# A third projection unit with its own buffers, and a hybrid attention/RWKV-7 kernel as one stretch instead of three

## The chip, the core and the metric

The kernel runs on one core of a Trainium2 chip. A core has TensorE (PE, matrix products into the PSUM banks), VectorE (DVE), ScalarE (ACT), GpSimd (POOL) and SyncE (SP, which here issues almost all DMA). Each runs its own instruction stream in order; they meet through semaphores. The metric is the device time of one execution in microseconds (us), lower is better. The median of three executions is given, and one further execution was profiled.

## The reference

`T` is 528 (16 meta tokens ahead of 512), `D` is 1024, 16 heads of 64, `D_FF` is 2816, all in fp32. Layer 0 mixes by stick-breaking attention, layer 1 by RWKV-7; each is followed by a SwiGLU.

```python
def swiglu(h, w_in, w_out):
    gate, up = jnp.split(jnp.einsum('btd,df->btf', h, w_in), 2, axis=-1)
    return jnp.einsum('btf,fd->btd', jax.nn.silu(gate) * up, w_out)

# attention, for each block of 128 queries
z = jnp.einsum('bhtd,bhsd->bhts', qb, kb).astype(jnp.float32) * scale
log_rest = jnp.where(mask, jax.nn.log_sigmoid(-z), 0.0)
later = lax.cumsum(log_rest, axis=3, reverse=True) - log_rest
att = jnp.where(mask, jnp.exp(jax.nn.log_sigmoid(z) + later), 0.0)
outs.append(jnp.einsum('bhts,bhsd->bhtd', att.astype(vb.dtype), vb))
...                                     # o: the outs put together
return jnp.einsum('btd,de->bte', o, w_o), v

# RWKV-7, after projections and small low-rank products
def step(S, inp):
    r_t, w_t, k_t, v_t, a_t, b_t = inp
    sa = jnp.einsum('bhij,bhj->bhi', S, a_t)
    S = (S * w_t[:, :, None, :] + sa[..., None] * b_t[:, :, None, :]
         + v_t[..., None] * k_t[:, :, None, :])
    return S, jnp.einsum('bhij,bhj->bhi', S, r_t)
...
y = ((y - mean) * lax.rsqrt(var + GN_EPS) * ln_x_w + ln_x_b)      # per head
bonus = jnp.sum(r_h * k_h * r_k, axis=-1, keepdims=True) * v_h
return jnp.einsum('btd,de->bte', (y + bonus) * g, w_o)

# the whole
for i in range(DEPTH):                  # DEPTH is 2; mix: attention, then RWKV-7
    h = h + mix
    h = h + swiglu(rms_norm(h, ffn_norm[i]), w_ffn_in[i], w_ffn_out[i])
return rms_norm(h[:, N_META:], final_norm)
```

## The kernel before

All activations are held with features on the partitions: 8 rows ("m" or "t", 0 to 7) of 128 features by the tokens. Every large product is made of *units*: a unit is 128 output features of one weight, so 1024 x 128 weights for the projections. fp32 accuracy comes from splitting each factor in a high and a low part and summing three products, hi x hi, lo x hi and hi x lo. A unit passes through five hands:

- SP loads it (`unit_load`, L770 ff) into `w_raw`, one of two buffers, unit u into buffer u % 2.
- ACT rounds it to `w_hi` (`split_hi`, L131), DVE subtracts for `w_lo` (`split_lo`, L135), again two buffers each.
- PE multiplies, for each row t, three matmuls for each stretch of columns (two stretches of 264 in layer 0, one of 512 in layer 1).
- DVE evicts the result from its PSUM bank; for a projection this is the residual addition (L1378), which frees the bank.

A buffer may be loaded again when both splits are made, and split again when PE is through with the unit that had it (`unit_done`).

The program is three `nc.Block`s. Each block has five functions, one for each engine, and at its end all engines meet before one of them enters the next:

1. Attention, first MLP half (`Mlp`, n = 0) and the front of the RWKV layer (`Front`: its projections and the tables of the recurrence).
2. The chunk stage (`chunk_stage`): the recurrence in chunks of 64 tokens.
3. `Output` (norm of each head, bonus, gate) and the second MLP half with the final norm (`Mlp`, n = 1).

Both MLP halves begin with the 8 units of the output projection `w_o`. The products of units 0 and 1 are woven into the stage ahead: as soon as a row of the attention output `o_hi`/`o_lo` (in layer 1 `x_hi`/`x_lo`) exists, PE multiplies it with both units. Unit 2 is split after unit 0 is done, since it has the same `w_hi`, `w_lo` buffers, and so on, in turn:

```python
        for m in range(KT):
            if m < 2:
                self.first.finish_out(pe, self, m)
                continue
            u = begin(m)
            products(m, range(KT), b.o_hi, b.o_lo, KT).then_inc(k.unit_done[u % 2].h, 1)
```

At the end of attention the last row exists only after the last pair of heads, so PE waits for `o_lo`, issues that row for units 0 and 1 (12 matmuls) and then unit 2. In `Output.tensor` a round m is: variance product of m, the head sums of m + 1, and the products of row m - 2 with units 0 and 1; rows 6 and 7 stand behind the loop.

The front needs constants: a mask over heads, two selection matrices `pick` and `put`, the chunk stage's masks. POOL makes them at the start of `Front.gpsimd` (L2572 ff), while PE is in the first units of the front. There ACT and DVE split v, the first projection's weights and the sums of the mixed inputs (L2033 and L2039).

In the chunk stage's block SP loads the two first units of `w_o`, then, when the gate is done, the residual `res` that the front had moved to DRAM, and waits for it ahead of the block's end:

```python
                sp.dma_start(k.res[:], k.res_kept).then_inc(res_in.h, 16)
                sp.wait_ge(res_in.h, 16)
```

Unit 2 and 3 of `w_o` are loaded behind that meeting, the units from 4 on when the buffers come free. The last front instruction on DVE is the product `bk` (L2570); the chunk stage's DVE stream begins with clearing `state` (L3044) and the product `neighbours` (L3056), on which PE's first chunk product (L3225) waits.

## Time and profile before

| | |
|---|---|
| median of 3 executions | 1543.97 us (1540.83 to 1547.42) |
| profiled execution, its own time | 1547.64 us |
| its span in the profile | 1545.7 us |
| TensorE busy | 1484.7 us, 96% of the span, 15443 matmuls |
| VectorE busy | 1024.0 us, 66% |
| ScalarE busy | 746.5 us, 48% |
| GpSimd busy | 104.9 us, 7% |
| DMA | 127.71 MB, mean 83 GB/s |
| mean granted TensorE clock | 0.992 of full |

The span runs from the first to the last instruction in the profile, and is 1.94 us shorter than the execution's own time. Busy times hold neither branches and semaphore instructions nor the issuing of DMAs. Matmuls are pipelined, so two neighbouring ones overlap in the profile, and the distance of their starts is what each costs. A timeline row has the start in us, the duration, engine, line, operation and tiles, and in brackets the idle time of that engine just ahead of it with what ended it; PEq is PE's sequencer. The granted clock is 1.00 at 2.4 GHz and 0.50 at 1.2 GHz.

### The profile page before, as it was taken

To read this page: it belongs to the slowest core of one execution; us is meant where nothing else is said; L and a number is where in the kernel's file an instruction comes from. 1 tells how busy PE (TensorE), PEld (TensorE's weight loads), DVE (VectorE), ACT (ScalarE), POOL (GpSimd) and SP (SyncE) were. 2 spreads that over 40 slices of the span, in tenths; PEclk is the share of its full clock that TensorE was granted. 3 is DMA by queue.
4 is the path that set the end of the run, shared out by engine and by line. 5 is a ranking of instruction groups with operands and counts; after the bars stand their busy time and mean duration, and the time that the engine had idled before them with its cause. 6 is when DMAs were issued, how large, how long until landed. Compare 5 with 4: busy or idle time off the path is not lost. (4 is left out here: it accounts for less than half of the span.)

```text
span 1545.7 us, 35328 instructions
## 1 busy us (share of the span) xinstructions
PE 1484.7 (96%) x15443; PEld 1364.5 (88%) x15443; DVE 1024.0 (66%) x1435; ACT 746.5 (48%) x1090; POOL 104.9 (7%) x145
## 2 busy tenths in 40 slices
PE   6999999999999999998999999999889999999997
PEld 6988898899999999998998788888558899899986
DVE  5675675687734886587788755545678885478732
ACT  4655555444522555467588433333344553245522
POOL 3110010000000001500000410101000000000010
PEclk9999999999999999998999999999999999999999
DMA  4212212324432333563222200000322434334331
GB/s 127 69 49 76 63 56 63 110 82 110 121 89 79 110 100 95 155 198 108 83 66 84 67 3 4 5 4 4 113 68 82 122 90 116 100 93 110 84 94 55
DMA packets 226840, 127.71 MB, mean 83 GB/s; under 512 B 8536, under 2 KB 221680, under 8 KB 226432
## 3 DMA queue, kind: packets, MB, share of 16 engines
q1 hardware_dynamic: 226384, 125.39, 28.3%
q8 instruction: 122, 2.00, 0.5%
q14 instruction: 30, 0.25, 0.1%
q10 hardware_dynamic: 304, 0.08, 0.0%
HBM read 119.03 MB, written 6.42 MB: 81 GB/s over the span
## 5 line engine op out<-in xcount | busy, mean ns | idle before, releaser
L131 ACT ACTIVATE w_hi<-w_raw 128x1024 fp32r<-128x1024 f32 (+1 forms) x124 | 143.8, 1160 | 221.1 <-PE psg L1844 115.4
L135 DVE TENSOR_TENSOR w_lo<-w_raw,w_hi 128x1024 fp32r<-128x1024 f32 (+1 forms) x123 | 167.9, 1366 | 69.8 <-ACT w_hi L131 69.7
L1844 PE MATMUL psg<-mid_hi_l,w_hi 128*128 128x264 f32 (+1 forms) x552 | 179.7, 325 | 3.1 <-DVE w_lo L135 2.2
L1844 PE MATMUL psg<-mid_lo_l,w_hi 128*128 128x264 f32 (+1 forms) x552 | 178.3, 323 | 0.0
L1844 PE MATMUL psg<-mid_hi_l,w_lo 128*128 128x264 f32 (+1 forms) x552 | 177.8, 322 | 0.0
L1844 PEld LDWEIGHTS psg<-mid_hi_l,w_hi 128*128 128x128 f32 x552 | 104.4, 189 | 12.2 <-DVE w_lo L135 2.8
L1844 PEld LDWEIGHTS psg<-mid_lo_l,w_hi 128*128 128x128 f32 x552 | 104.5, 189 | 8.0 <-issue 0.2
L1844 PEld LDWEIGHTS psg<-mid_hi_l,w_lo 128*128 128x128 f32 x552 | 104.5, 189 | 7.9
L2640 PE MATMUL psg<-x_hi,w_hi 128*128 128x264 f32 (+1 forms) x320 | 100.7, 315 | 7.1 <-DVE w_lo L135 7.1
L1378 DVE TENSOR_TENSOR res<-res,psg 128x512 f32<-128x512 f32 (+1 forms) x38 | 26.3, 692 | 119.2 <-PE psg L1844 103.5
L2640 PE MATMUL psg<-x_lo,w_hi 128*128 128x264 f32 (+1 forms) x320 | 99.7, 311 | 0.0
L2640 PE MATMUL psg<-x_hi,w_lo 128*128 128x264 f32 (+1 forms) x320 | 99.5, 311 | 0.0
L2640 PEld LDWEIGHTS psg<-x_hi,w_hi 128*128 128x128 f32 x320 | 61.8, 193 | 11.3 <-DVE w_lo L135 8.1
L1687 PE MATMUL psx<-t_hi_l,x_sums_hi_l 128*128 128x264 f32 (+1 forms) x240 | 67.7, 282 | 0.0
L1687 PE MATMUL psx<-t_lo_l,x_sums_hi_l 128*128 128x264 f32 (+1 forms) x240 | 67.7, 282 | 0.0
L1687 PE MATMUL psx<-t_hi_l,x_sums_lo_l 128*128 128x264 f32 (+1 forms) x240 | 67.5, 281 | 0.0
L2640 PEld LDWEIGHTS psg<-x_hi,w_lo 128*128 128x128 f32 x320 | 61.9, 193 | 2.7
L2640 PEld LDWEIGHTS psg<-x_lo,w_hi 128*128 128x128 f32 x320 | 61.8, 193 | 2.5
L582 PE MATMUL psg<-x_hi,w_hi 128*128 128x264 f32 x200 | 60.6, 303 | 2.6 <-DVE w_lo L135 2.2
L1090 ACT ACTIVATE x_sums_hi_l<-x_sums_l 128x1024 fp32r<-128x1024 f32 x40 | 41.9, 1057 | 33.9 <-DVE x_sums_l L1267 33.9
L582 PE MATMUL psg<-x_hi,w_lo 128*128 128x264 f32 x200 | 57.6, 288 | 0.0
L582 PE MATMUL psg<-x_lo,w_hi 128*128 128x264 f32 x200 | 57.3, 286 | 0.0
(517 smaller groups left out, 4767.6 us busy)
## 6 DMA issues: line engine op xcount, KB each, us to landing
w_raw<-in_w_ffn_out_dram SPq DMA_DIRECT2D x40, 704.0 KB, 4.6
w_raw<-in_w_qkv_dram SPq DMA_DIRECT2D x24, 512.0 KB, 3.8
w_raw<-in_w_rkv_dram SPq DMA_DIRECT2D x24, 512.0 KB, 4.1
x_raw_l<-in_w_ffn_in_dram SPq DMA_DIRECT2D x18, 512.0 KB, 4.2
x_raw_l<-in_w_ffn_in_dram SPq DMA_DIRECT2D x36, 256.0 KB, 4.8
w_raw<-in_w_ffn_in_dram SPq DMA_DIRECT2D x16, 512.0 KB, 3.8
y_raw_l<-in_w_ffn_in_dram SPq DMA_DIRECT2D x16, 512.0 KB, 4.1
y_raw_l<-in_w_ffn_in_dram SPq DMA_DIRECT2D x32, 256.0 KB, 4.7
```

Source lines behind the costliest of these rows:

```text
L131: k.nc.scalar.activation(k.w_hi[j][:, 0:kt, :], k.raw[j][:, 0:kt, :], ACT.Copy).then_inc(k.hi_ready[j].h, 1)
L135: k.nc.vector.tensor_tensor(k.w_lo[j][:, 0:kt, :], k.raw[j][:, 0:kt, :], k.w_hi[j][:, 0:kt, :].bitcast(F32), ALU.subtract).then_inc(k.lo_r ...
L582: done = mm(out, w[:, t, :], x, start=t == 0 and n == 0, stop=t == KT - 1 and n == 2)
L1090: self.k.nc.scalar.activation(p.s_hi[:, part], p.s[:, part], ACT.Copy).then_inc(self.s.high_s.h, 1)
L1378: nc.vector.tensor_tensor(row, row, self.psum(i % 2), ALU.add).then_inc(self.freed(i), 1)
L1687: done = self.k.nc.tensor.matmul(out, w[:, t, :], x_part[:, t, :], start=start and t == 0 and n == 0, stop=t == KQ - 1 and n == 2, skip_gr ...
L1844: done = k.nc.tensor.matmul(self.bank(i, c), w[:, t, :], x, start=t == 0 and n == 0, stop=t == count - 1 and n == 2)
L2640: done = nc.tensor.matmul(k.psg[:, 2 * j + c, 0:size], w[:, t, :], x[:, at:at + size], start=t == 0 and a == 0, stop=t == KT - 1 and a == 2)
```

## The change

**A third unit.** Unit 2 of `w_o` gets buffers of its own (`third_hi`, `third_lo`) and a PSUM bank of its own in both MLP halves, so neither waits for units 0 and 1. ACT splits it in the last pair of heads ahead of its eviction of `o_hi`, and in `Output` in round 0 between the square and the logarithm; DVE splits it ahead of `o_lo`, and in `Output` behind `product(2)`. At the end of attention PE multiplies rows 0 and 1 of unit 2 (12 matmuls), then the last row of units 0 and 1, then rows 2 to 7. At the end of `Output` rows 5 to 7 of units 0 and 1 stand behind the loop; ahead of them PE multiplies rows 0 to 4 of unit 2 (15), behind them rows 5 to 7 (9). The buffers of the units that follow are assigned as before, the PSUM banks of some are exchanged (`slot`).

**Constants.** `Front.constants` stands in POOL's stream of the first MLP half now, behind the release of the last of that half's paired units; only the cast of `put` stays at the start of the front. Four tiles (`put_raw`, `raw_first`, one hi and one lo tile of the paired weights) have other addresses.

**One block.** One `nc.Block` holds all stages. `chunk_stage` returns its five functions instead of running them. In place of the meetings stand semaphores: `c_first_v` and `c_first_p` (DVE's and POOL's last front products), `psum_free` of the front's last unit ahead of the first chunk products, and the chunk stage's own `y_r` and `bk_r` ahead of `Output`. SP still waits for `res` before it goes on to the units 2 and 3 of `w_o`.

```diff
@@ attention, ACT (DVE alike with third_low)
             if not last:
                 unit_hi(k, act, 3 * p + 5, KT)
+            else:
+                self.out.third_high(act)
             act.wait_ge(self.out_d.h, p + 1)
@@ attention, PE
+    def finish(self, pe, out):
+        out.third(pe, range(2))
         pe.wait_ge(self.olo_r.h, PAIRS)
-        out.out_part(pe, i, KT - 1)
+        for i in range(2):
+            out.out_part(pe, i, KT - 1)
+        out.third(pe, range(2, KT))
@@ class Mlp
+    def third_high(self, act):
+        k, u = self.k, self.u0 + 2
+        act.wait_ge(k.raw_loaded[0].h, 16 * (u // 2 + 1))
+        if self.n == 0:
+            act.wait_ge(k.unit_done[1].h, u // 2 - 1)
+        k.nc.scalar.activation(self.b.third_hi[:], k.raw[0][:, 0:KT, :], ACT.Copy).then_inc(k.hi_ready[0].h, 1)
+
+    def third(self, pe, rows):
+        k, u = self.k, self.u0 + 2
+        pe.wait_ge(k.lo_ready[0].h, u // 2 + 1)
+        for t in rows:
+            for c in range(len(self.spans)):
+                done = self.part(pe, 2, t, self.b.o_hi, self.b.o_lo, KT, c)
+        if KT - 1 in rows:
+            done.then_inc(k.unit_done[0].h, 1)
...
@@ Mlp.scalar (Mlp.vector alike)
         for m in range(KT):
-            self.hi(act, m + 2)
+            if m:
+                self.hi(act, m + 2)
@@ Mlp.gpsimd
         self.first.release(pool)
+        if not self.tail:
+            self.wait_of(pool, self.s.four, FIRST_PAIRS - 1)
+            self.nxt.constants(pool)
@@ chunk_stage, SP
-        with nc.Block() as block:
-            @block.sync
-            def _(sp):
+        def sync(sp):
+            sp.wait_ge(ch.first_v.h, 1)
...
@@ class Output, ACT (DVE alike, with its wait for bk_r at the head)
             nc.scalar.activation(self.sq[q], self.center[q], ACT.Square).then_inc(self.sq_r.h, 1)
+            if m == 0:
+                self.out.third_high(act)
             act.wait_ge(self.var_d.h, m + 1)
@@ class Output, PE
         lag = 2
+        pe.wait_ge(self.chunks.y_r.h, CHUNKS - 1)
         head_sums(0)
         for m in range(KT):
             variance(m)
             if m < KT - 1:
                 head_sums(m + 1)
-            if m >= lag:
+            if lag <= m < KT - 1:
                 rows(m - lag)
-        for m in range(KT - lag, KT):
+        pe.wait_ge(self.bon_r.h, KT - 1)
+        out.third(pe, range(THIRD_ROWS))
+        for m in range(KT - lag - 1, KT):
             rows(m)
+    def finish(self, pe, out):
+        out.third(pe, range(THIRD_ROWS, KT))
```

What stands in a row on PE at the end of attention, before. L671 is the last value product, `o_hi` and `o_lo` are the attention output, `w_hi` and `w_lo` the weights; L1844 is units 0 and 1, L791 unit 2.

```order
L671 MATMUL psg<-rest_68,vtok 64x16
L1844 MATMUL psg<-o_hi,w_hi 128x264
L1844 MATMUL psg<-o_lo,w_hi 128x264
L1844 MATMUL psg<-o_hi,w_lo 128x264
...
L1844 MATMUL psx<-o_hi,w_hi 128x264
L1844 MATMUL psx<-o_lo,w_hi 128x264
L1844 MATMUL psx<-o_hi,w_lo 128x264
L791 MATMUL psg<-o_hi,w_hi 128x264
```

The same place in the changed kernel (L678 is the last value product, L1881 all units, `third_...` the third unit's buffers):

```order
L678 MATMUL psg<-rest_68,vtok 64x16
L1881 MATMUL psg<-o_hi,third_hi_l_147 128x264
L1881 MATMUL psg<-o_lo,third_hi_l_147 128x264
L1881 MATMUL psg<-o_hi,third_lo_l_148 128x264
...
L1881 MATMUL psg<-o_hi,w_hi 128x264
L1881 MATMUL psg<-o_lo,w_hi 128x264
L1881 MATMUL psg<-o_hi,w_lo 128x264
...
L1881 MATMUL psg<-o_hi,third_hi_l_147 128x264
```

12 matmuls of unit 2 moved ahead of the 12 of units 0 and 1; its other 36 follow these.

On PE at the end of the output stage, before: L3628 is a variance product, and 18 matmuls of rows 5 to 7 lie between it and unit 2.

```order
L1844 MATMUL psg<-x_hi,w_lo 128x512
L3628 MATMUL psg<-aa,heads 128x512
L1844 MATMUL psg<-x_hi,w_hi 128x512
L1844 MATMUL psg<-x_lo,w_hi 128x512
L1844 MATMUL psg<-x_hi,w_lo 128x512
...
L1844 MATMUL psg<-x_hi,w_lo 128x512
L791 MATMUL psg<-x_hi,w_hi 128x512
```

And in the changed kernel (L3691 is the last variance product):

```order
L1881 MATMUL psg<-x_hi,w_lo 128x512
L3691 MATMUL psg<-aa,heads 128x512
L1881 MATMUL psx<-x_hi,third_hi_l_200 128x512
L1881 MATMUL psx<-x_lo,third_hi_l_200 128x512
L1881 MATMUL psx<-x_hi,third_lo_l_201 128x512
...
L1881 MATMUL psg<-x_hi,w_hi 128x512
...
L1881 MATMUL psx<-x_hi,third_hi_l_200 128x512
...
L1881 MATMUL psg<-x_hi,w_hi 128x512
```

15 matmuls of unit 2 moved in behind the last variance product, the 18 of rows 5 to 7 follow, then the other 9 of unit 2 and unit 3.

On ACT at the border of chunk and output stage, before: `xn<-psg` is the last eviction of the recurrence's output, `aa<-psx` the square of round 0, `aa<-psx,eps` its logarithm.

```order
L131 ACTIVATE w_hi<-w_raw 128x1024 x2
L2997 ACTIVATE xn<-psg 128x8x64
L2930 UNCONDITIONAL_BRANCH
L1861 UNCONDITIONAL_BRANCH
L3541 ACTIVATE aa<-psx 128x512
L3546 ACTIVATE aa<-psx,eps 128x512
L3548 ACTIVATE aa<-aa 128x512
L3541 ACTIVATE aa<-psx 128x512
```

And in the changed kernel, where L945 is the split of the third unit:

```order
L131 ACTIVATE w_hi<-w_raw 128x1024 x2
L3042 ACTIVATE xn<-psg 128x8x64
L3599 ACTIVATE aa<-psx 128x512
L945 ACTIVATE third_hi_l_200<-w_raw 128x1024
L3606 ACTIVATE aa<-psx,eps 128x512
L3608 ACTIVATE aa<-aa 128x512
L3599 ACTIVATE aa<-psx 128x512
```

The two branches are gone, and a weight split stands between the first square and the first logarithm.

## Rows read from the trace of the kernel before

**Rows 1.** The page: its span, and the granted clock in 40 equal slices, in tenths.

```profile
span 1545.7 us, 35328 instructions
...
PEclk9999999999999999998999999999999999999999
```

**Rows 2.** Timeline of TensorE, end of attention: start, duration, instruction, [idle before <-what ended it].

```profile
274.72 0.39 PE L1844 MATMUL psg<-o_hi,w_hi 128*128 128x264 f32 x1 [1.58 <-DVE o_lo L499]
...
278.19 0.39 PE L791 MATMUL psg<-o_hi,w_hi 128*128 128x264 f32 x1 [1.75 <-DVE w_lo L135]
```

**Rows 3.** Timeline of VectorE behind it; then the DMA issued at 278.1 to 278.6.

```profile
284.42 0.70 DVE L1378 TENSOR_TENSOR res<-res,psg 128x528 f32<-128x528 f32 x1 [3.18 <-PE psg L791]
...
290.20 0.70 DVE L1378 TENSOR_TENSOR res<-res,psg 128x528 f32<-128x528 f32 x1 [2.17 <-PE psg L791]
...
w_raw<-in_w_o_attn_dram SPq DMA_DIRECT2D x1, 512.0 KB, 6.2
```

**Rows 4.** One line of the front's splits: duration in ns, min/median/max, and starts.

```profile
L2039 DVE TENSOR_TENSOR v_lo<-v_raw,v_hi x1: 1942/1942/1942, 617.9 to 617.9; 128x1024 fp32r<-128x1024 f32 x1
L2039 DVE TENSOR_TENSOR w_lo<-w_raw,w_hi x1: 1217/1217/1217, 727.3 to 727.3; 128x1024 fp32r<-128x1024 f32 x1
```

**Rows 5.** Stretches: length, busy us (count) of each engine, granted clock, DMA share, GB/s.

```profile
600.00:640.00 40.00, 37.21 (x289) 36.66 (x288) 21.29 (x26) 16.75 (x22) 24.38 (x51) 0.96 0.44 120
...
618.40:621.80 3.40, 1.51 (x13) 1.30 (x12) 3.40 (x4) 2.32 (x3) 3.26 (x3) 1.00 0.03 8
621.80:625.20 3.40, 3.40 (x16) 3.40 (x17) 2.31 (x2) 0.49 (x2) 3.26 (x3) 0.51 0.65 190
...
1147.50:1150.90 3.40, 3.40 (x9) 2.67 (x8) 1.49 (x2) 0.98 (x2) 0.00 (x0) 0.50 1.15 305
```

**Rows 6.** Timelines of VectorE and TensorE, last front instruction and first chunk product.

```profile
880.49 1.77 DVE L2570 TENSOR_TENSOR bk<-kk_in,w_inv 128x512 f32<-128x512 f32 x1
...
883.86 0.53 PE L3225 MATMUL psg<-bk,ar 64*64 64x64 f32 x11 [2.19 <-DVE neighbours L3056]
```

**Rows 7.** The border of chunk and output stage: SyncE, ScalarE, VectorE, TensorE; two DMA landings.

```profile
1093.10 0.34 SPq L2941 DMA_DIRECT2D res<-res_kept  x1
...
res<-res_kept SPq DMA_DIRECT2D x1, 2112.0 KB, 10.5
...
1099.49 1.99 ACT L131 ACTIVATE w_hi<-w_raw 128x1024 fp32r<-128x1024 f32 x2
...
1107.83 0.69 ACT L3546 ACTIVATE aa<-psx,eps 128x512 f32<-128x512 f32 x1 [1.22 <-PE psx L3628]
...
1100.57 2.36 DVE L135 TENSOR_TENSOR w_lo<-w_raw,w_hi 128x1024 fp32r<-128x1024 f32 x2 [3.28 <-ACT w_hi L131]
...
1110.82 0.74 DVE L3567 SCALAR_TENSOR_TENSOR aa<-psx,vec,aa 128x512 f32<-128x512 f32 x1
...
1104.03 0.67 PE L3618 MATMUL psx<-xn,center 128*128 128x512 f32 x1 [2.26 <-PEq L2930]
...
w_raw<-in_w_o_rwkv_dram SPq DMA_DIRECT2D x1, 512.0 KB, 4.8
```

**Rows 8.** Timelines of TensorE and VectorE, end of output stage and units 2 and 3.

```profile
1135.81 1.02 PE L3628 MATMUL psg<-aa,heads 128*128 128x512 f32 x2
...
1141.17 0.50 PE L1844 MATMUL psg<-x_hi,w_hi 128*128 128x512 f32 x1 [1.36 <-DVE x_lo L3579]
...
1145.99 0.50 PE L791 MATMUL psg<-x_hi,w_hi 128*128 128x512 f32 x1 [1.78 <-DVE w_lo L135]
...
1158.99 0.69 DVE L1378 TENSOR_TENSOR res<-res,psg 128x512 f32<-128x512 f32 x1 [1.92 <-PE psg L791]
...
1164.55 0.69 DVE L1378 TENSOR_TENSOR res<-res,psg 128x512 f32<-128x512 f32 x1 [0.78 <-PE psg L791]
```

**Rows 9.** Timeline of VectorE in the first MLP half, late output units.

```profile
442.81 1.62 DVE L135 TENSOR_TENSOR w_lo<-w_raw,w_hi 128x1408 fp32r<-128x1408 f32 x1 [0.77 <-ACT w_hi L131]
...
449.40 0.70 DVE L1378 TENSOR_TENSOR res<-res,psg 128x528 f32<-128x528 f32 x1 [4.97 <-PE psg L1844]
```

More of the change, by code:

```diff
@@ L496, in vector @@
                 evict(3 * p + 4, 0)
+            else:
+                self.out.third_low(dve)
             dve.wait_ge(self.ohi_r.h, p + 1)
@@ L781, in unit_lo @@
     split_lo(k, j, kt)
-def unit_products(k, pe, u, rows, spans, x_hi, x_lo, first, last):
-    j = u % 2
-    for c, (at, size) in enumerate(spans):
-        for t in rows:
-            hi, lo = x_hi[:, t, at:at + size], x_lo[:, t, at:at + size]
-            for n, (w, x) in enumerate(((k.w_hi[j], hi), (k.w_hi[j], lo), (k.w_lo[j], hi))):
-                done = k.nc.tensor.matmul(k.psg[:, 2 * j + c, 0:size], w[:, t, :], x,
-                                          start=t == first and n == 0, stop=t == last and n == 2)
-    return done
 PLAIN = 4
@@ L1761, in begin, with products @@
             return u
[L1763 to L1769 removed]
+        def products(i, rows, x_hi, x_lo, count):
+            for c in range(len(self.spans)):
+                for t in rows:
+                    done = self.part(pe, i, t, x_hi, x_lo, count, c)
+            return done
+        self.first.finish(pe, self)
+        for m in range(3, KT):
             u = begin(m)
```

1068 lines of the change are left out of this document (551 added, 517 removed).

## The prediction

> **What bounds the kernel now.** I read the page first: the span and its clock line [rows 1]. PE is in use nearly everywhere, and its clock line is at 9 (full, 2.4 GHz) but for a few slices at 8. So a change can win only where PE stands still or runs at 1.2 GHz. The next view is PE's timeline at the four places that the diff touches, since each of its idle gaps carries in brackets what ended it: the end of attention [rows 2], the start of the RWKV front, the border between front and chunk stage, and the border between chunk stage and output stage with the projection behind it. The last view is a table of short stretches with the granted clock [rows 5]: it shows what a gap costs after it is over.
>
> **The change, part by part.**
>
> *Third unit at the end of attention.* Before, PE ends the value products at 273.14 (274.72 less 1.58), waits 1.58 us for o_lo, issues 12 matmuls (the last row of units 0 and 1), and waits 1.75 us for the split weights of unit 2 [rows 2]. One unit of 48 such matmuls takes 5.8 us (the residual additions stand 284.42 and 290.20 [rows 3]), 0.12 us a matmul. In the new order 12 matmuls of unit 2 stand ahead of the first wait (1.45 us, beside the wait for o_lo), then the 12, then the other 36. Unit 3 then begins at 274.72 + 48 x 0.121 = 280.5; before it began at 278.19 + 5.8 = 284.0. That is 3.5 us less. The split itself costs ACT 1.0 (two in 1.99 [rows 7]) and DVE 1.2 us [rows 4], while both wait for the value products. What is late next is a load: that of unit 4 is queued on SP behind the first pair's three loads, which wait for unit 1, as before. It is issued near 278.1 and lands 6.2 us later [rows 3], 284.3; with both splits (2.3 us with the hand-over) unit 4 is ready at 286.6, and PE wants it at 280.5 + 5.8 = 286.3. I take 0.3 back: -3.2. The idle time that would be left to pay is bounded by the two gaps (3.3 us) on one side, and by 0 if the load is what sets the pace, on the other.
>
> *Constants.* POOL builds masks and tables, 24.38 us of work in the slices of 600 to 640 [rows 5], beside the front's first splits. There DVE's v_lo takes 1942 ns, and the same form later, with POOL idle, 1217 [rows 4]. v_lo is followed by a residual addition and the split that PE then waits for, so 0.7 us come off that wait. The Trainium skill (SBUF — State Buffer, section "SBUF: two separate sides") says that VectorE and GpSimd share a port pair as an exclusive lock. This stretching agrees with it. What stays in this place is one copy (put), which runs while DVE waits. After that wait the clock is granted at 0.51 over 621.8 to 625.2, and the stretch before has PE busy 1.51 of 3.40 [rows 5]. Half speed over 3.4 us of dense matmuls costs 1.7 us. The wait ahead of it, 1.9 us of those 3.4, gets shorter by 0.7, and I take it that no dip follows: -1.7 in this execution, with 0 as the other end.
>
> *Front to chunk stage.* All engines meet behind DVE's bk product (880.49 and 1.77 long, so 882.26); the clearing of the state and the neighbours product follow, PE starts at 883.86 [rows 6]. Without the meeting the clearing starts 0.5 us earlier, nothing else on that chain moves: -0.55. POOL's first product of the chunk stage now comes up against DVE's; bounds are 0 (it blocks the neighbours product for as long) and -1.0 (also the zeroing of the tiles, which is then 0.9 earlier, counts).
>
> The same skill's page Runtime: NRT & Kernel Launch, section "Instruction fetch mechanics", warns that a taken branch out of the fetched pages stalls the fetch. Were it so here, each removed stage entry would give some more; but PE resumes 0.4 us after the landing of res at the later border [rows 7], and that holds meeting and branch together.
>
> *Chunk stage to output stage, third unit there.* The meeting here does not wait for an engine but for SP's res load, issued 1093.1 and landing 10.5 later, 1103.6; PE starts 1104.03 [rows 7]. PE, ACT and DVE now pass it; DVE ends its weight splits at 1102.9, so the first two sums come 1.2 us earlier. But SP still waits for res, and the third unit's load is behind that wait. Issued at 1103.65 with 4.8 to landing [rows 7] it is there at 1108.45. ACT now waits for it in order, between the first square and the first logarithm, and DVE between two products. So that logarithm, before at 1107.83, comes at 1108.5 + 1.0 = 1109.5. DVE has its own split (1.2) and two held back instructions (1.3) ahead of the first finishing step: 1112.1 where it was 1110.82 [rows 7]. All later rounds follow it, so the whole stage is 1.3 us later, not earlier. At its end PE waits for x_lo ahead of row 5 and of row 6 (1.36 in the one shown), then 1.78 for w_lo of unit 2 [rows 8]; 24 matmuls of the third unit now fill this. They take 0.232 us each (24 in 5.56 us, from 1158.99 to 1164.55 [rows 8]). The last variance product begins at 1135.81, is through PE's queue near 1136.7 and is 1.3 later now, 1138.0. 15 third matmuls (3.5) and the 18 of rows 5 to 7 (4.2) end at 1145.7, and x_lo of row 6 is there in time (1141.17 + 1.3 = 1142.5, wanted at 1142.9). So unit 1 is done at 1145.7, where it was 1144.2 (1145.99 less 1.78), and the last 9 matmuls (2.1) end at 1147.8. Unit 3 needs, from unit 1's end, x_hi and a square on ACT (1.3) and two splits (2.2) and starts near 1149.2. Before: unit 2 at 1145.99 and unit 3 at 1145.99 + 5.56 = 1151.6. That is -2.4. Again a load is next: SP issues the pair's loads when unit 1 is done (now 1145.7), the load of unit 4 1.7 us behind them, and with the same 6.2 us as [rows 3] and 2.3 of splits unit 4 is ready at 1155.9; PE wants it at 1149.2 + 5.56 = 1154.8, and before it began at 1157.1. So -1.2 is left. Bounds: -4.5 (the load lands before ACT asks) and +2 (landing 3 us later).
> The clock was at 0.50 over 1147.5 to 1150.9 in this execution [rows 5], 1.7 us lost. The gap in the new order is 1.4 against 1.78, and it may dip as well; I count half, -0.8. At the first border the gap is 1.7 instead of 2.19 [rows 6]; I count 0.3 there by the same reasoning.
>
> **Sum.** -3.2 - 0.7 - 0.55 - 1.2 = -5.65 in waits, and -1.7 - 0.8 - 0.3 = -2.8 in clock. From the profiled execution's own 1547.64 (span 1545.7 and 1.94 around it) that gives 1539.2. That execution is 3.7 above the median of the runs shown (1543.97), and I take part of that for dips that other executions don't have; with less than half of the clock term, the median gives 1543.97 - 5.65 - 1.2 = 1537.1. Between them: 1538.2.
>
> **Rivals.**
> *A. The output stage really starts early.* The load of the third unit lands before ACT needs it (bandwidth is free then), or ACT's wait is caught up by the gaps in PE's first three rounds. Then the 1.2 us at the start stay and the last load is earlier too: -4.5 in place of -1.2, 1534.9. For it: ACT is idle 1.22 ahead of that logarithm [rows 7], so the first rounds have slack. Against: the load starts only after 1103.6, whatever the stage does, and the 4.8 us are measured there.
> *B. Loads take back what the reordering gives.* Unit 4 is late at both places. If both loads land a further 2 us late (four loads of one queue share bandwidth there), the waits move from the splits to the landing, and 1.5 to 2 us go at each place: 1542.
> *C. Slower: the constants hold DVE in the MLP.* POOL's chain now stands beside the output units of the first half, from about 435 on. The place is DVE's weight split at 442.81, for the unit that PE begins when the one before it is through, just ahead of the residual addition at 449.40 [rows 9]. By the same lock, it can be held by a POOL instruction. The split ends at 444.4, so its slack is 4.9 us; below this it costs nothing. If DVE were held for the whole 24.4 us, 19.5 would come through: 1543.97 - 5.65 + 19.5 = 1558. Against: v_lo, in the midst of the same chain, was held by 0.7 us, not more.
> That the change doesn't do what it says is part of B: the meetings go, but the loads behind them set the same times.
>
> **How the numbers follow.** A measurement of this kernel tells 0.5% (7.7 us) from no change, so faster is below 1536.3, slower above 1551.7. Forecast (1535 to 1541.5) 0.61, A 0.19, B 0.16, C 0.04. Faster: A 0.18 and the low end of the forecast 0.14, 0.32. Slower: 0.03. No change that can be told: 0.65. The range goes from the middle of A to the far side of B, 1533 to 1543.5.
>
> **What would show it.** Right: 12 matmuls with third weights ahead of the wait for o_lo, and a gap under 0.5 us there; no PE wait for w_lo near 276, but a short one before unit 4. v_lo at 1.2 us and clock at 1.0 behind it. PE's first chunk product 2.2 less 0.5 us after the front's last matmul. ACT idle at the first third split of the output stage until the landing, near 5 us after res, and the row products of that stage later relative to its start by more than 2 us. A PE wait of about 1.4 before unit 3 and of about 1 before unit 4. Wrong: no ACT wait at that split (A), unit 4 more than 2 us late (B), or DVE instructions of 3 us and more near 435 to 455 with PE waiting (C).

## The result and the profile after

| | before | changed |
|---|---|---|
| median (executions) | 1545.65 us (18) | 1535.23 us (18) |
| lowest to highest | 1540.55 to 1552.09 | 1530.87 to 1547.77 |
| ratio, 95% interval | | 0.9939, 0.9923 to 0.9954 |
| profiled: own time, span | 1547.64, 1545.7 | 1536.88, 1534.9 |

The changed kernel is 0.61% faster by the ratio, 9.4 us on 1545.65; the two medians are 10.4 us apart. The median lies inside the forecast range, nearer its low end than its middle. Two further sets of executions gave the changed kernel 0.9929 (0.9902 to 0.9957) and 0.9952 (0.9927 to 0.9977). The page after, first its span, then busy times, granted clock and one DMA queue (packets, MB, share of 16 engines), answers to [rows 1]:

```profile
span 1534.9 us, 35309 instructions
...
PE 1480.9 (96%) x15443; PEld 1359.0 (89%) x15443; DVE 1023.2 (67%) x1436; ACT 746.7 (49%) x1090; POOL 100.2 (7%) x145
...
PEclk9999999999999999999999999999899999999999
...
q8 instruction: 122, 2.00, 0.5%
```

PE is busy 3.8 us less and the span is 10.8 us shorter, so about 7 us of that difference were idle time of PE, the rest is mostly clock. The table under the experiments shows how much of such a difference between two single profiles is chance.

**End of attention.** TensorE after, which answers to [rows 2]; then VectorE's timeline there, for [rows 3]:

```profile
272.85 0.27 PE L678 MATMUL psg<-rest,vtok 128*64 128x16 f32 x4
273.05 0.39 PE L1881 MATMUL psg<-o_hi,third_hi_l 128*128 128x264 f32 x1
...
274.70 0.39 PE L1881 MATMUL psg<-o_hi,w_hi 128*128 128x264 f32 x1
```

```profile
285.46 1.23 DVE L135 TENSOR_TENSOR w_lo<-w_raw,w_hi 128x1024 fp32r<-128x1024 f32 x1 [3.79 <-ACT w_hi L131]
...
287.91 0.70 DVE L1409 TENSOR_TENSOR res<-res,psg 128x528 f32<-128x528 f32 x1
```

The third unit's matmuls start 0.2 us behind the last value product, and the 12 of units 0 and 1 follow without a wait at 274.70, nearly where they began before (274.72), with 12 of unit 2's 48 already done. From the end of the value products to the end of the wait for `mid_lo` at the front it was 273.14 to 615.18, 342.04 us; now it is 273.05 to 612.19, 339.14 us. The difference is 2.9. The w_lo row shows the load that is late next: the split of unit 4 ends at 286.68, and PE begins it at 286.75 after 0.1 us of idle time.

**Head of the front and the place where the constants went.** VectorE's `v_lo`, PE's wait behind it and the 3.4 us from there, for [rows 4, 5]:

```profile
614.73 1.23 DVE L2083 TENSOR_TENSOR v_lo<-v_raw,v_hi 128x1024 fp32r<-128x1024 f32 x1 [2.60 <-ACT v_hi L2077]
...
617.88 0.39 PE L1881 MATMUL psg<-mid_hi_l,w_hi 128*128 128x264 f32 x1 [1.03 <-DVE w_lo L135]
...
617.90:621.30 3.40, 3.40 (x28) 3.40 (x29) 1.90 (x2) 0.83 (x2) 0.00 (x0) 1.00 0.60 178
```

`v_lo` takes 1.23 us in place of 1.94, PE's wait behind it is 1.03 in place of 1.89, and the clock behind it is full. In the first MLP half, POOL's longest selection beside VectorE's weight split, then the busy times of 40 us (PE, PEld, DVE, ACT, POOL), for [rows 9]:

```profile
439.99 1.72 POOL L2635 TENSOR_SCALAR_AFFINE_SELECT pick_raw<-pick_raw 128x256 f32<-128x256 f32 x1
...
439.72 1.68 DVE L135 TENSOR_TENSOR w_lo<-w_raw,w_hi 128x1408 fp32r<-128x1408 f32 x1 [0.78 <-ACT w_hi L131]
...
425.00:465.00 40.00, 40.00 (x328) 39.88 (x327) 15.56 (x17) 10.19 (x11) 18.46 (x51) 1.00 0.32 91
```

Here it is POOL that is held: the select takes 1.72 us, where the three of the same form ahead of it took 0.45 each, and it ends 0.3 us behind the split. The split takes 1.68 us where it took 1.62 before. PE is busy for all of the 40 us. Rival C did not happen.

**First border.** PE's first chunk product, for [rows 6]: 1.73 in place of 2.19.

```profile
876.60 1.11 PE L3274 MATMUL psg<-bk,ar 64*64 64x64 f32 x31 [1.73 <-DVE neighbours L3103]
```

**Second border.** SyncE's issue of `res` and its landing time, three rows of PE's timeline, and the 10.2 us behind, for [rows 7]:

```profile
1082.55 0.45 SPq L2987 DMA_DIRECT2D res<-res_kept  x1
...
res<-res_kept SPq DMA_DIRECT2D x1, 2112.0 KB, 10.7
...
1086.84 0.88 PE L3391 MATMUL psx<-wt,xt 64*64 64x64 f32 x23 [0.91 <-issue]
...
1091.10 0.62 PE L3396 MATMUL psg<-ar,state 64*64 64x64 f32 x13 [2.57 <-issue]
...
1093.61 1.22 PE L3681 MATMUL psx<-xn,center 128*128 128x512 f32 x1 [0.69 <-ACT xn L3042]
...
1093.70:1103.90 10.20, 8.91 (x10) 2.93 (x10) 3.15 (x5) 3.42 (x5) 0.00 (x0) 0.55 0.37 103
```

The same gap in the last chunk, before:

```profile
1100.01 0.68 PE L3347 MATMUL psg<-ar,state 64*64 64x64 f32 x15 [0.98 <-issue]
```

This place did not go as forecast. PE stands for 2.57 us in the last chunk with `issue`, which means that no engine and no DMA of the program releases it; before, that gap was 0.98. The load of `res` stands in the same place in both: it is issued 4.3 us ahead of the product `psx<-wt,xt` of the last chunk (L3391 of the changed kernel, L3342 of the one before). So PE enters the output stage at 1093.61, 0.36 us behind the landing of `res` (1093.25), although it does not wait for it any more. And for most of the next 10 us it runs at half clock. In the middle of the gap the DMA queues look like this (1088 to 1090: packets, MB, share of 16 engines):

```profile
q1 hardware_dynamic: 50, 0.84, 99.9%
q8 instruction: 1, 0.02, 3.0%
```

The queue with `res` has all engines, and one packet of the queue `instruction` is in between. On the page that queue has 122 packets and 2.00 MB, 16.4 KB a packet, and the count does not change with the kernel. The packet ahead of this one came at 1080.60, just before `res`; this one runs from 1088.67 to 1089.63, and PE goes on 1.47 us behind its end.

**End of the output stage.** The last head sum's eviction on VectorE, PE's waits before units 3 and 4, ScalarE's wait for the load of unit 4, and unit 5's residual addition, for [rows 8]:

```profile
1128.45 0.69 DVE L3648 TENSOR_TENSOR bonus<-psg,vv 128x512 f32<-128x512 f32 x1 [0.66 <-PE psg L3683]
...
1141.88 0.51 PE L1881 MATMUL psg<-x_hi,w_hi 128*128 128x512 f32 x1 [1.50 <-DVE w_lo L135]
...
1148.47 0.50 PE L1881 MATMUL psg<-x_hi,w_hi 128*128 128x512 f32 x1 [0.74 <-DVE w_lo L135]
...
1146.10 1.06 ACT L131 ACTIVATE w_hi<-w_raw 128x1024 fp32r<-128x1024 f32 x1 [4.34 <-DMA w_raw<-in_w_o_rwkv_dram]
...
1159.92 0.69 DVE L1409 TENSOR_TENSOR res<-res,psg 128x512 f32<-128x512 f32 x1 [0.58 <-PE psg L1881]
```

The waits before units 3 and 4 were forecast as 1.4 and 1.1; they are 1.50 and 0.74. The clock, 0.50 over 1147.5 to 1150.9 before, is full here.

### The profile page after: what moved, and what is told of

Read it like the earlier page. It is cut to its first block, busy times and chain, and to the rows that moved or that the text cites. A ratio compares the mean times of both kernels' runs of the same rounds, so it can differ in the third digit from the quotient of the medians.

```text
span 1534.9 us, 35309 instructions
## 1 busy us (share of the span) xinstructions
PE 1480.9 (96%) x15443; PEld 1359.0 (89%) x15443; DVE 1023.2 (67%) x1436; ACT 746.7 (49%) x1090; POOL 100.2 (7%) x145
## 4 chain that ended last, share of the span: by engine, by line
PE 82%; DVE 9%; ACT 5%; issue 2%; DMA 1%; SPq 0%; DVEq 0%; ACTq 0%
PE psg L1881 25%; PE psx L1722 13%; PE psg L1722 11%; PE psg L2687 8%; PE psg L3343 2%; PE psg L3362 2%; PE psg L589 2%; DVE w_lo L135 2%; PE psx L589 2%; PE psx L3309 2%; PE psg L617 1%; PE psg L673 1%; ACT rest_hi L329 1%; DVE rest_lo L428 1%; DVE sum_lo L445 1%
## 5 line engine op out<-in xcount | busy, mean ns | idle before, releaser
L131 ACT ACTIVATE w_hi<-w_raw 128x1024 fp32r<-128x1024 f32 (+1 forms) x122 | 141.6, 1162 | 210.2 <-PE psg L1881 145.6
L1881 PE MATMUL psg<-mid_hi_l,w_hi 128*128 128x264 f32 (+1 forms) x720 | 232.8, 323 | 2.2 <-DVE w_lo L135 1.3
L1881 PE MATMUL psg<-mid_lo_l,w_hi 128*128 128x264 f32 (+1 forms) x720 | 231.6, 322 | 0.0
L1881 PE MATMUL psg<-mid_hi_l,w_lo 128*128 128x264 f32 (+1 forms) x720 | 231.0, 321 | 0.0
L1881 PEld LDWEIGHTS psg<-mid_hi_l,w_hi 128*128 128x128 f32 x720 | 135.3, 188 | 14.1 <-DVE w_lo L135 2.0
L1881 PEld LDWEIGHTS psg<-mid_lo_l,w_hi 128*128 128x128 f32 x720 | 135.3, 188 | 10.5 <-issue 0.2
L1881 PEld LDWEIGHTS psg<-mid_hi_l,w_lo 128*128 128x128 f32 x720 | 135.4, 188 | 10.3
L1722 PE MATMUL psx<-t_hi_l,x_sums_hi_l 128*128 128x264 f32 (+1 forms) x240 | 67.6, 282 | 0.0
L1120 ACT ACTIVATE x_sums_hi_l<-x_sums_l 128x1024 fp32r<-128x1024 f32 x40 | 41.9, 1057 | 33.8 <-DVE x_sums_l L1298 33.8
```

Source lines behind the costliest of these rows:

```text
L131: k.nc.scalar.activation(k.w_hi[j][:, 0:kt, :], k.raw[j][:, 0:kt, :], ACT.Copy).then_inc(k.hi_ready[j].h, 1)
L1120: self.k.nc.scalar.activation(p.s_hi[:, part], p.s[:, part], ACT.Copy).then_inc(self.s.high_s.h, 1)
L1722: done = self.k.nc.tensor.matmul(out, w[:, t, :], x_part[:, t, :], start=start and t == 0 and n == 0, stop=t == KQ - 1 and n == 2, skip_gr ...
L1881: done = k.nc.tensor.matmul(self.bank(i, c), w[:, t, :], x, start=t == 0 and n == 0, stop=t == count - 1 and n == 2)
```

## The experiments

Each run was profiled once. The table holds what of the program can be compared over all fourteen profiles: PE's wait for w_lo at the head of the front, its wait for `neighbours` at the first border, the issue gap in the last chunk (L3396 of the changed kernel), and the time from PE's product `psx<-wt,xt` ahead of it (L3391) to unit 5's residual addition on VectorE. "Half" stands where the granted clock fell behind the wait, or inside the last stretch.

```
kernel                       w_lo        neighbours  issue gap  L3391 to unit 5
before                       1.89 half   2.19 half   0.98       72.7 half
before, second profile       1.90 half   2.18 half   0.71       72.1 half
changed                      1.03        1.73        2.57       73.1 half
changed, a2                  1.09        1.73        1.60       72.2 half
changed, a3                  1.06        1.73 half   1.74       68.4
u1 three stretches           1.22        2.18 half   0.98       70.8 half
u2 constants back            1.89        1.73        2.41       69.2
u3 attention third late      1.19        1.73        1.47       68.5
u4 output third late         1.03        1.73        0.37       70.0
v1 border and output only    1.90 half   1.73        2.29       68.5
v2 attention only            1.90        2.18 half   1.92       76.1 half
t1 dummy traffic             1.11        1.73        1.74       69.3
n1 res behind units          1.09        1.73 half   none       67.8
n2 the same again            1.12        1.73        none       67.6
```

In profiles of one and the same kernel the waits for engines repeat to 0.1 us or better. The issue gap does not, and the half clock does not: within these few profiles it is partly chance, and it came more often behind the longer wait.

The table leaves out most of the chunk stage, whose stream on PE is the same in all, but for one or two instructions. From PE's first chunk product to L3391 it took 213.5 and 217.7 us in the two profiles of before, 210.2, 214.4 and 216.6 in the three of the changed kernel, and up to 222.7 in u3 (223.3 in t1, with its copies). Most of the difference is half clock: beyond 890 us there is none in the first profiles of before and changed, in v1 and in v2, 17 us in the second of before, and 31 us in u3, of which one stretch is

```profile
983.50:1000.60 17.10, 17.10 (x326) 15.27 (x324) 7.83 (x15) 1.58 (x3) 2.50 (x2) 0.50 0.01 2
```

Between 695 and 730 us every profile has 3.4 to 10.3 us at half clock (10.2 and 10.3 in the two of before, 6.9, 3.4 and 6.8 in the three of the changed kernel). So the times of two single profiles tell nothing of an effect of 3 us; single waits, and ratios over many executions, do. The ratios given are not those of the medians and differ from them by up to 0.0013.

**u1, three stretches again.** All engines meet ahead of and behind the chunk stage:

```diff
-        with nc.Block() as block:
-            ...
+        stretch([att.sync, mlp.sync, front.sync], ...)
+        stretch([chunks.sync], ...)
+        stretch([last.sync, ...], ...)
```

> The changed kernel with three stretches again: all engines meet ahead of the chunk stage and behind it; third unit and constants stay as changed. Theory (the border gives little in waits, the time moved with code and clock): PE's first chunk product stands 2.2 us behind the front's last matmul instead of 1.73, 0.5 us lost; at the border to the output stage PE starts 0.4 us behind the landing of res, as in both kernels (1104.03 behind 1103.6, 1093.61 behind 1093.25). The 2.57 us issue gap of PE at the end of the chunk stage and the 10 us at half clock behind it (1093.7 to 1103.9 in the changed kernel) belong to the place of the code and go or stay by chance; if they go, this kernel is not slower than the changed one: ratio to before 0.993 to 0.996. Rival (removing the meetings is itself worth the 3 us by which the changed kernel beats the forecast): ratio 0.996 to 0.998, all of the loss between 880 and 1105.

0.9961 (0.9941 to 0.9982), against 0.9939 for the changed kernel. The table shows 2.18 at the first border and half clock behind it. At the second, PE starts 0.5 us behind the landing of `res`, as the theory has it, and L3391 to unit 5 took 70.8, 2.4 more than the changed kernel at full clock; 1.7 of these are a half-clock stretch of 3.4 us. The issue gap is 0.98. The theory's "not slower" is not borne out, though the intervals overlap; the rival's size fits, but more than half of it is clock.

**u2, constants back at the head of the front.**

```diff
@@ Mlp.gpsimd
-            self.nxt.constants(pool)
@@ Front.gpsimd
+        self.constants(pool)
         nc.gpsimd.tensor_copy(r.put[:], r.put_raw[:])
```

> The changed kernel with POOL's constants back at the head of the front. Theory (VectorE's splits are stretched while POOL works, and the clock falls behind the longer wait): v_lo takes 1.9 us again instead of 1.2, PE's wait for w_lo there is 1.9 instead of 1.03, the granted clock is 0.5 for 3.4 us behind it; 0.8 + 1.6 = 2.4 us slower than the changed kernel, ratio to before 0.9955. Rival (the dip is chance, only the stretch returns): 0.8 us, 0.9944, and clock 1.0 behind the wait.

0.9929 (0.9901 to 0.9958), not told from the changed kernel; neither the theory's 0.9955 nor the rival's 0.9944 can be told from it either. `v_lo`'s duration, PE's wait and the stretch behind it:

```profile
L2080 DVE TENSOR_TENSOR v_lo<-v_raw,v_hi x1: 1820/1820/1820, 613.9 to 613.9; 128x1024 fp32r<-128x1024 f32 x1
...
617.69 0.39 PE L1878 MATMUL psg<-mid_hi_l,w_hi 128*128 128x264 f32 x1 [1.89 <-DVE w_lo L135]
...
617.70:621.10 3.40, 3.40 (x28) 3.40 (x29) 2.36 (x2) 0.55 (x2) 3.26 (x3) 1.00 0.63 178
```

The stretch of the split and the wait of 1.89 return, so these 0.86 us are the constants' place. The dip does not return: the clock is 1.00 behind the same wait, as the rival has it. Two other rows of this run, PE's issue gap and ScalarE's split of the third unit:

```profile
1095.92 0.68 PE L3394 MATMUL psg<-ar,state 64*64 64x64 f32 x14 [2.41 <-issue]
...
1102.34 1.06 ACT L945 ACTIVATE third_hi_l<-w_raw 128x1024 fp32r<-128x1024 f32 x1 [1.35 <-DMA w_raw<-in_w_o_rwkv_dram]
```

The issue gap is there again (2.41), and as PE kept its full clock here, ScalarE shows its wait for the third unit's load, 1.35 us, as the forecast had it; in the changed kernel's first profile the half clock hid it.

**u3, the attention's third unit late.**

```diff
@@ Attention, ACT (DVE alike)
-            else:
-                self.out.third_high(act)
@@ Mlp.scalar (Mlp.vector alike)
+            elif not self.tail:
+                act.wait_ge(k.unit_done[0].h, (self.u0 + 2) // 2)
+                self.third_high(act)
@@ Attention.finish
-        out.third(pe, range(2))
         pe.wait_ge(self.olo_r.h, PAIRS)
         ...
-        out.third(pe, range(2, KT))
+        out.third(pe, range(KT))
```

> The changed kernel with the third unit of the first MLP half split behind the end of unit 0 and multiplied behind units 0 and 1, as before; it keeps its own buffers. Theory: PE's waits of 1.58 (o_lo) and 1.75 (w_lo) return, 3.3 us there, and 3.1 at the first paired unit: ratio to before 0.996. Rival (the load of unit 4 would take the gain back anyway): under 1.5 us.

0.9971 (0.9947 to 0.9994), 2.9 to 6.5 us slower than the changed kernel by its three ratios. PE's waits are back as 1.58 and 1.69. VectorE's residual additions of units 2 and 3:

```profile
284.45 0.43 DVE L1399 TENSOR_TENSOR res<-res,psg 128x264 f32<-128x264 f32 x1 [3.13 <-PE psx L1881]
...
290.23 0.70 DVE L1407 TENSOR_TENSOR res<-res,psg 128x528 f32<-128x528 f32 x1 [2.17 <-PE psg L1881]
```

They stand where those of before stood [rows 3], and at the front's wait for w_lo the program is 3.4 us late against the changed kernel (621.26 for 617.88). Over all fourteen profiles, from the start of the last value product to the end of the front's wait for `mid_lo`, it is 342.2 or 342.3 us in the four where the third unit is late there (both of before, u3 and v1) and 339.0 to 339.3 in the other ten.

**u4, the output stage's third unit late.** As u3, in `Output` and for `self.tail`; rows 0 to 7 of units 0 and 1 stand ahead of all 24 matmuls.

> The changed kernel with the third unit of the second MLP half split behind unit 0 and multiplied behind rows 0 to 7 of units 0 and 1, as before (own buffers; one wait of DVE for res is added, which its order held before). Theory A (the weaving is worth what the traces show: 24 matmuls in gaps of 1.3, 1.4 and 1.8 us, and about 1.2 us lost to the load of unit 4): 3 to 4 us slower than the changed kernel, ratio 0.996. Rival B (the third split on ACT and DVE at the head of the stage holds its first rounds by as much): no difference, ratio 0.994, first rounds 1.3 us earlier.

0.9959 (0.9933 to 0.9984), 3.1 us slower than the changed kernel's 0.9939, but the intervals overlap. PE's waits of 1.31, 1.47 and 1.73 are back. From the last head sum's eviction to unit 5's residual addition:

```profile
1129.00 0.69 DVE L3654 TENSOR_TENSOR bonus<-psg,vv 128x512 f32<-128x512 f32 x1 [0.64 <-PE psg L3687]
...
1162.95 0.69 DVE L1412 TENSOR_TENSOR res<-res,psg 128x512 f32<-128x512 f32 x1 [0.58 <-PE psg L1888]
```

That is 33.95 us, in the changed kernel 31.47 (1128.45 to 1159.92), so the weaving is worth 2.5 us there. At the head of the stage u4 gets back part of it: from the first such eviction to the fourth it took 11.7 us, at full clock 12.2 in the changed kernel (a3), 11.9 in v1 and 12.3 in u2. So theory A, less some 0.5 us of B. The issue gap in the last chunk is only 0.37 us here, though `res` is issued at the same place as in the changed kernel: the stall is a matter of chance in its length too.

**v2 and v1, one side of the change each.** v2 joins the edits of u1, u2 and u4, v1 those of u2 and u3.

> Only the third unit at the end of attention is left of the change: three stretches, constants at the head of the front, the output stage's third unit late. Theory (its 2.9 us come through to the end, and nothing else in the program moves): ratio to before 0.998, PE's wait for w_lo at the head of the front 1.9 again, for neighbours 2.18, and half clock behind both. Rival (shifting the program by 3 us is enough to lose the dips that both profiles of the kernel before show at 618 to 625, 884 to 888 and 1147 to 1153): one or more of the three is missing, ratio 0.996.

> The changed kernel with constants at the head of the front and the third unit at the end of attention late: left are the one stretch and the third unit in the output stage. Theory (the stretch gives 0.45 in waits at the first border, the output stage up to 3 but only where the code fetch at its head does not stall): ratio to before 0.9965 to 0.998. Rival (the border gives most of the gain, by the clock behind it): 0.994 to 0.996.

v2 0.9963 (0.9944 to 0.9982), v1 0.9961 (0.9936 to 0.9986). For v2 the rival's 0.996 came out, and the theory's 0.998 is at the edge of the interval; v1 lies just below its theory's range, and its interval holds both. The profile of v2 misses two of the three dips (head of the front and units 2 to 3) and has a new one of 13 us at the second border, behind an issue gap of 1.92. v1 has the dip at the head of the front, PE's wait and the stretch behind it being

```profile
620.83 0.48 PE L1878 MATMUL psg<-mid_hi_l,w_hi 128*128 128x264 f32 x1 [1.90 <-DVE w_lo L135]
...
621.80:625.20 3.40, 3.40 (x20) 3.40 (x20) 1.40 (x1) 0.00 (x0) 3.27 (x3) 0.62 0.90 252
```

so half clock came behind this wait in both profiles of before and in v1, and not in u2 and v2. The two halves, 5.7 and 6.0 us by their ratios, add up to more than the whole, within their intervals of 3 to 4 us each way. In v2 only some 3 us of waits at the end of attention and the 0.6 behind unit 5 (below) were taken out; that its other 2 us are rarer half clock is not shown.

**a2, b2 and a3, the same kernels again.**

> The changed kernel itself, profiled a second time. Theory: what belongs to the program returns to 0.2 us: no PE wait at the end of attention, 1.03 for w_lo at the head of the front, 1.73 for neighbours, the 2.57 us issue gap at L3396, PE's issue gaps at the same instructions. What is chance moves: the stretches at half clock. Rival (the clock's stretches belong to the program too): half clock again at 707 to 712 and 1093.7 to 1103.9, and nowhere else.

> The kernel before itself, profiled a second time. Theory: waits of 1.58 and 1.75 at the end of attention, 1.89 at the head of the front, 0.98 at L3347 and the 2.26 at the border return; the stretches at half clock (618 to 625, 704 to 707, 714 to 721, 884 to 888, 1147 to 1151) stand at least partly elsewhere. Rival: all five return at their places, so that the missing ones of the changed kernel are its gain.

> The changed kernel itself, for comparison in the same call and a third profile. Theory: ratio 0.9935; stall of 1.6 to 2.6 us at L3396 and half clock from 1094 for 8 to 10 us, as in its two other profiles. Rival: the half clock there was chance and is missing.

0.9929 for a2, 0.9952 for a3, and 1550.23 us for the single execution of before. The waits return as the theory says. The gap in the last chunk returns too, but between 1.6 and 2.6 us in these three. Of half-clock stretches, all five of before (at 621, 704, 714, 884 and 1147) returned in its second profile, which is that run's rival, with a sixth of 17 us at 986; in the changed kernel's three the one at the second border came in two, and one at the first border in one. Neither "all chance" nor "all program" holds.

**t1, dummy traffic.** Three copies of 2112 KB in the chunk stage that nobody waits for:

```diff
@@ chunk_stage, SP
+            for n in (2, 4, 6):
+                sp.wait_ge(dx_d.h, level_count(n, levels - 2))
+                sp.dma_start(nc.dram_tensor(f'spare{n}', [P, KT, T], F32).ap(), k.res_kept)...
```

> The changed kernel with three further copies of 2112 KB from DRAM to DRAM in the chunk stage, behind the inversions of chunks 2, 4 and 6 (their results are used by nobody). Nothing waits for them. 
1.0033 (1.0012 to 1.0053), against 0.9929 for the changed kernel beside it: about 16 us by the ratios, 13.7 by the medians, for traffic that nothing waits for, and far more than the 2 to 6 of the theory. The first copy's issue and landing time, then PE's longest issue gaps:

```profile
939.08 0.53 SPq L2986 DMA_DIRECT2D spare<-res_kept  x1
...
spare<-res_kept SPq DMA_DIRECT2D x1, 2112.0 KB, 9.7
...
947.63 0.69 PE L3278 MATMUL psg<-bk,ar 64*64 64x64 f32 x9 [3.15 <-issue]
...
1001.11 0.27 PE L3387 MATMUL psg<-state,ar 64*64 64x64 f32 x2 [2.13 <-issue]
...
1049.80 0.91 PE L3278 MATMUL psg<-bk,ar 64*64 64x64 f32 x13 [3.13 <-issue]
```

The copies run from 939.1 to 948.8, 990.7 to 1000.8 and 1041.5 to 1051.0, and in or right behind each PE stands for 2.1 to 3.2 us, at instructions before which the changed kernel has no gap of 0.5. Each gap ends 1.3 to 1.4 us behind the end of a packet of the queue `instruction`, and that packet started 7.6 to 7.7 us behind the one ahead of it. PE's issue gaps between 880 and 1086 add up to 16.0 us, 7.9 in the changed kernel. The clock is at half from 945.6 to 952.4 and from 1048.0 to 1054.8, from inside the first and the third gap on.

**n1 and n2, res behind the units.** The order of loads at the end of the chunk stage is turned; PE's stream is the same, instruction for instruction:

```diff
@@ chunk_stage, SP
-            sp.dma_start(k.res[:], k.res_kept).then_inc(res_in.h, 16)
-            sp.wait_ge(res_in.h, 16)
@@ Mlp.sync
             if i == 3:
+                if self.tail:
+                    sp.dma_start(self.k.res[:], self.k.res_kept).then_inc(self.first.chunks.res_in.h, 16)
@@ Mlp.vector
+        if self.tail:
+            dve.wait_ge(self.first.chunks.res_in.h, 16)
         for m in range(KT):
             residual(m, m)
```

> The changed kernel with the loads at the end of the chunk stage in another order: units 2 and 3 of w_o first, the 2112 KB of res behind them and SP not waiting for it (DVE waits ahead of its first residual addition). TensorE's stream is the same, instruction for instruction. 
> The kernel with res loaded behind units 2 and 3 once more, beside the changed kernel in the same call. Theory (from L3391 to unit 5's residual it took 67.8 us where the changed kernel took 73.1 and 72.2, and this belongs to the program): 4 us under the changed kernel, that is ratio 0.990 where the changed one has 0.993, and again no issue gap over 0.5 at L3396 and full clock over the border. Rival (the clock gives it back elsewhere): no difference between the two, and half-clock stretches at other places of the same sum.

n1 0.9926 (0.9899 to 0.9953), n2 0.9920 (0.9896 to 0.9943); medians 1534.85 and 1534.38 where the changed kernel, beside them, had 1537.36 and 1539.56. Of n1: the issue of `res`, PE's rows around the last chunk and into the output stage, the 10.2 us from there, and ScalarE's third split:

```profile
1099.06 1.12 SPq L1082 DMA_DIRECT2D res<-res_kept  x1
...
1093.08 1.05 PE L3393 MATMUL psx<-wt,xt 64*64 64x64 f32 x29 [0.91 <-issue]
...
1095.34 0.34 PE L3404 MATMUL psg<-arm,uv 128*64 128x64 f32 x4 [0.21 <-ACT uv L3022]
...
1097.71 1.12 PE L3684 MATMUL psx<-xn,center 128*128 128x512 f32 x2 [1.22 <-ACT xn L3044]
...
1097.70:1107.90 10.20, 7.95 (x16) 2.63 (x16) 8.19 (x11) 4.91 (x8) 0.00 (x0) 1.00 0.87 313
...
1101.87 1.06 ACT L945 ACTIVATE third_hi_l<-w_raw 128x1024 fp32r<-128x1024 f32 x1 [0.77 <-DMA w_raw<-in_w_o_rwkv_dram]
```

Between L3393 and the last chunk product there is no issue gap any more. With one stretch and `res` loading, eight profiles have one there of 0.37 to 2.57 us, seven of them of 1.47 and more; with three stretches and `res` loading, four have 0.71 to 1.92; without the load two have none. The clock over the border is full. ScalarE still waits for the third unit, 0.77 us here and 0.53 in n2, where the theory had no wait. L3391 to unit 5 takes 67.8 and 67.6 us, the shortest of all. So the effect of bulk traffic on the gap is shown from both sides: by adding traffic in other chunks, and by taking it away with the same stream. This version beats before by 0.7 to 0.8%; against the changed kernel its time is lower both times (by the ratios 0.5 and 5 us), but by less than the intervals can tell. The ratio of n1 is nearer to its rival's 0.993 than to its theory's 0.991.

**That the gaps are fetches of code.** The traces settle this. Number the instructions of PE's own stream (products, weight loads and what stands for semaphores) as each trace lists them: the last chunk's gap stands before number 26050 in every kernel. From 890 us up to it the fourteen profiles have 117 issue gaps of 0.5 us and more at which PE waits for no semaphore, besides the one of 0.91 before L3391 that each has. All 117 stand a multiple of 256 instructions from number 26050, or one instruction ahead of such a place, and all end 1.2 to 1.6 us behind the end of a packet of the queue `instruction`. Under the load of `res` the packet that ends the last chunk's gap starts 6.0 to 8.1 us behind the one ahead of it (twelve profiles, 8.1 in the changed kernel's first), without it 5.0 and 5.4; in the chunk stage the median distance is 4.0 to 4.3. The gap of 0.91 before L3391 is the same in all fourteen, with `res` loading and without, and belongs to something else.

## Why the prediction was right, and where its sizes were off

- *End of attention, -3.2.* Measured -2.9 in the changed kernel, and back in u3 and v1. The step that a load becomes the next bound was right: ScalarE waits for the load of unit 4 and splits it from 284.37, the forecast had the landing at 284.3.
- *Constants, -0.7 in the wait.* Measured -0.86, and back in u2, v1 and v2 with 1.89 or 1.90. *-1.7 in clock* was too sure: with a wait of 1.9 the clock fell in 3 of 5 profiles, with 1.03 to 1.22 in none of 9. As an expected value it is nearer -1 (three fifths of 1.7).
- *First border, -0.55.* Measured -0.46. The clock behind it was sized too small: with 2.18 it fell in 4 of 4 profiles, with 1.73 in 2 of 10. The forecast gave 0.3 for that; these odds give nearer 1.4 (one stretch of 3.4 us at half costs 1.7). The four profiles with 2.18 are also those with a meeting, so the two are not told apart.
- *Second border: "DVE ends its weight splits at 1102.9, so the first two sums come 1.2 us earlier".* This step failed in the changed kernel. It took for granted that PE is free once the engines it waits for are; the code fetch of PE held it. In n1, n2 and u4, where that gap is absent or 0.37 us, the stage starts 4.6 us behind L3391, in the changed kernel's three profiles 6.8, 6.4 and 5.9 (before: 6.6 and 6.0).
- *"The whole stage is 1.3 us later".* Wrong by size: ScalarE does wait for the load (1.16 in a3, 1.35 in u2, 0.93 in v1), but the rounds have slack that takes most of it: at full clock the first three rounds take 11.9 to 12.3 us, 0.2 to 0.6 more than the 11.7 of before.
- *The weave, -2.4 at unit 3 and -1.2 from unit 4 on.* From the last head sum to unit 5 it went from 35.5 us, 33.8 without its half-clock stretch, to 31.5: -2.3. The forecast's own figure for that part is -1.2 - 1.3 = -2.5, and its waits of 1.4 and 1.1 were 1.50 and 0.74.
- *Rival B* was right in its cause (both times a load is next) and not in its size; *rival A* came true in part. In the changed kernel at full clock (a3) the gaps of the first rounds do catch up ScalarE's wait, and in n1 and n2 L3391 to unit 5 is 3.3 us shorter than before's 71.0, not 4.5. *Rival C* did not happen.

In waits alone, then: 2.9 + 0.86 + 0.46 + 2.6 (71.0 to 68.4 from L3391 to unit 5: 72.7 less 1.7 for its half-clock stretch, and a3 at full clock) + 0.6 (unit 5 to the end: 375.6 in both profiles of before, 374.9 to 375.0 in every other run, v2 too; its cause is open) = 7.4 us, against 5.65 forecast; the term that was mis-sized is the output stage's, -1.2 for -2.6. What is left of the 9.4 is clock, 2 us net: three places where dips became rarer, less the new one at the second border, which took 3.8 and 4.7 us (72.2 and 73.1 against 68.4) in two of three profiles. The net figure is worked out from few profiles and has the uncertainty of the ratio, 2.4 us each way.

That the median fell inside the range owes something to luck. The forecast was a gain of 5.8 us and the measured one is 9.4, or 10.4 by the medians; the three executions that it started from have a median 1.7 us below that of all eighteen, which moved the forecast time towards the measured one. The stall and the half clock at the second border, which it did not have, also hid a part of what it had sized too small. And it gave 0.65 to a change too small to be told, taking 0.5% as the least that a measurement tells; the measured change is 0.61%.

## What to carry to other kernels

When a meeting of engines is removed, ask what it hid beside the wait that the trace names: here it was a stall for TensorE's own code, 0.98 and 0.71 us in the two profiles of before, where PE then waited for `res` anyway. Put a bulk load where TensorE works through few instructions or waits anyway (in n1, under `res`, it had 16 products in 10.2 us and no issue gap), and look for `issue` gaps under it, since nothing in the program's own order tells of them. Count a wait by its length and by the clock that it may cost behind it, and take the second as a chance from several profiles of the same kernel, since one profile shows only one draw.

## What the runs showed of the hardware that was not expected

- TensorE's code comes over the same DMA engines as the data. At the same place in PE's stream the gap was 0.37 to 2.57 us in twelve profiles under a load of 2112 KB and absent in two without it, and copies of that size set gaps of 2.1 to 3.2 us where there were none. All 117 issue gaps of 0.5 us and more that were compared stand at steps of 256 of PE's instructions and end 1.2 to 1.6 us behind a packet of the queue `instruction`, so this queue carries PE's code; its 122 packets of 16.4 KB are one for every 253 of PE's 30,886 matmuls and weight loads, and one for every 257 of its instructions if the 474 others in the trace are counted. The Trainium skill (Runtime: NRT & Kernel Launch, section "Instruction fetch mechanics") says that crossing a code block's boundary costs one tail-bump, "mostly hidden". Here it was not: in the chunk stage, with its many small matmuls, 6.4 to 9.4 us of issue gaps stand between 880 and 1086 even without the copies of t1 (before 8.4 and 7.0, n1 6.4, n2 9.4).
- The half clock came more often behind longer waits: in 3 of 5 profiles behind 1.9 us at the head of the front, in 4 of 4 behind 2.18 at the first border, in 2 of 10 behind 1.73 there. It moved between profiles of one kernel while every wait for an engine at these places stayed within 0.1 us. It goes with much of why executions of one kernel lie up to 17 us apart (1530.87 to 1547.77): the slowest has a mean granted clock of 0.985, the fastest 0.993, and 0.008 of 1540 us are 12 us.
